# A hybrid decoder trunk in one core: the input loaded in halves with its first products begun block by block, and the last tile's final norm done token by token

## The chip, the core and the metric

One core of a Trainium2 chip runs the whole program in one launch. The metric is the device time of one execution in microseconds; the time of a kernel is the median over its executions. Engines are named as in the profile: PE is TensorE, DVE is VectorE, ACT is ScalarE, POOL is GpSimd, SP is SyncE, which here only issues DMAs.

## What is computed

A step of a two-layer trunk over 512 prompt tokens and 8 sample tokens of width 1024, all in float32. Each layer is a recurrent mixer followed by a retrieval layer (PEER), and the result goes through one more norm:

```python
def rmsnorm(x, w):
    xf = x.astype(jnp.float32)
    y = xf * lax.rsqrt(jnp.mean(xf * xf, axis=-1, keepdims=True) + EPS)
    return (y * w.astype(jnp.float32)).astype(x.dtype)
```

Layer 0 does norm, an input projection, gated DeltaNet and Mamba-2 side by side, an output projection and a residual add. Layer 1 does the same with GLA. In each layer the retrieval picks, for every token, 128 experts (8 heads, 16 each) out of 16384. The row of an expert holds a vector u and a vector v of 1024 numbers each. The token's output is the sum over its experts of gate * gelu(u . h) * v, which is added to x.

## The kernel before

**Layout.** Everything before the retrieval is kept with the channels on the partitions: `xT` is (128, 8, 520), 8 blocks of 128 channels by 512 prompt and 8 sample tokens. The tokens are worked in two pairs of tiles: columns 0 to 255, and 256 to 519. A projection (`gemm`, PE) reads weight blocks of 128x1024 (0.52 MB each), which SP loads into a ring of 3 slots, and makes 8 products per block, each of them two MATMUL instructions in the profile. The results stand in PSUM banks 2 and 3 by turns; block b waits until the bank of block b-2 was read (`gemm_free`). ACT and DVE read them out.

**Start.** SP issues 12 loads (`NLOADS`), all counted by one semaphore, `params`: the masks (of which `ones` and `ident` are two planes), the whole of `xT`, and the small tensors, the last of them `a_log`; then the weight blocks. PE, ACT and DVE wait for all 12 (L982, L1322, L1906). Then comes the first norm, over `xT[:, :, 0:256]`: ACT squares 8 channel blocks (L1090), DVE adds them up one by one (L1414), PE sums over the partitions by a product with `ones` (L564), ACT takes the root (L1103), DVE its reciprocal and then scales the 8 channel blocks into `hT` (L1424). The first projection waits for all 8 (`h_ready`, L627).

**Order of work.** From then on a unit is one tile of 128 tokens in one layer; 8 units follow one another, the last being tile 3 of layer 1. A unit is a loop over 128 picks (136 in tile 3's, which take the 8 sample tokens in as 8 further picks). Pick g: POOL gathers 128 rows of 8 KB by an indirect DMA into one of 7 ring slots, DVE makes the dot product with `htok` (L2168), ACT the gate and a diagonal matrix of it, PE two products (half a row of v each, 4 MATMUL instructions) that add into PSUM banks 0 and 1. A slot is free again when PE is done (`v_done`). In units 0 to 5 some picks' v is added by DVE instead. The mixers of later tiles, the choice of experts and the final norms of earlier tiles are cut into pieces, each with a due pick, and run between the picks (`front`, `choose`). In the last unit nothing of this is left but the picks.

**End of a unit.** ACT copies the sum out of PSUM into `otok`, PE turns it by 8 transposes (L1076), for tile 3 also the sample tokens' columns by 8 small ones (L1080), and DVE adds it to `xT` (L2142). The final norm is again squares, sums, product, root, reciprocal, 8 scalings into `y_out`, and POOL stores that with one DMA (L527). For tile 3 with the sample tokens (136 columns, `FINAL[2]`) all of this comes after the last pick, as nothing else is left. POOL then waits for all stores.

## Time and profile before

| | |
|---|---|
| median of 3 runs | 3461.0 us (3457.2 to 3465.04) |
| the profiled execution's own time | 3458.52 us |
| its span in the profile | 3456.7 us |
| TensorE's mean granted clock | 0.938 of full speed |
| busy | PE 2853.8 (83%), DVE 2331.4 (67%), ACT 1210.4 (35%), POOL 1265.8 (37%) |
| DMA | 1225.42 MB, mean 355 GB/s; DMA engines' busy share by fortieths of the span: 4204697998999899999999999999999899999996 |
| chain that ended last | PE 44%, DMA 27%, DVE 16%, ACT 5%, issue 4% |

The profile is of one execution, whose span leaves out 1.8 us that its own time has. A busy time is of one engine; a share of the chain says how much of the span the end of the kernel hung on that engine's work or on a transfer. "Idle before" in a row of the timeline is how long the engine had nothing to do before it, and what ended that.

### The profile page before, as it was taken

Reading aid. Unit: us, or ns where it says so; the run is one execution under the profiler, and the core shown is the slowest. Engines: PE = TensorE matmul, PEld = TensorE weight load, DVE = VectorE, ACT = ScalarE, POOL = GpSimd, SP = SyncE. Lnnn points to the kernel's source line nnn. Section 1 sums busy time; section 2 is a strip of 40 time slices with the busy share of each in tenths; the row PEclk is TensorE's granted clock in tenths of the full one; section 3 lists DMA queues with packets and bytes.
Section 4 is the critical chain, followed back from the end, with each engine's and each line's share of the span. In section 5 each row is a group of like instructions: output and inputs, shape, how many; then the busy total and the mean of one; then the engine's idle time right before and its main releaser. Section 6 shows DMA issues by size and latency. Waiting matters only on the chain.

```text
span 3456.7 us, 31768 instructions
## 1 busy us (share of the span) xinstructions
PE 2853.8 (83%) x9796; PEld 1642.4 (48%) x9796; DVE 2331.4 (67%) x5015; ACT 1210.4 (35%) x3536; POOL 1265.8 (37%) x1102
## 2 busy tenths in 40 slices
PE   7879897888997788797988898787788787787886
PEld 6767664555564256454642356354355232322222
DVE  3453788786767888687566787766667776755444
ACT  3211355332333343433333432432323343333333
...
DMA  4204697998999899999999999999999899999996
GB/s 148 80 1 143 238 359 300 358 365 362 407 413 420 367 406 382 384 386 387 411 421 421 389 406 381 361 343 412 369 413 420 349 419 421 386 422 419 421 422 268
DMA packets 183660, 1225.42 MB, mean 355 GB/s; under 512 B 21185, under 2 KB 21585, under 8 KB 48194
## 3 DMA queue, kind: packets, MB, share of 16 engines
...
## 4 chain that ended last, share of the span: by engine, by line
PE 44%; DMA 27%; DVE 16%; ACT 5%; issue 4%; DVEq 2%; POOL 1%; SPq 0%; POOLq 0%; ACTq 0%
PE ps L562 43%; DMA ring<-in_uv,picked 25%; DVE ring L2168 5%; DVE otok L2133 1%; ACT diag L1088 1%; ACT scratch L1088 1%; DVEq L1974 1%; POOL ring L547 1%; DVE scratch L1937 1%; ACT gated L1088 1%; DMA out_o_gla<-scratch 1%; ACT L1088 1%; ACT act_v L1088 1%; DVE scratch L1941 0%; DVE scratch L1955 0%
## 5 line engine op out<-in xcount | busy, mean ns | idle before, releaser
L562 PE MATMUL ps<-ring,diag 128*128 128x512 f32 (+1 forms) x3380 | 1712.9, 639 | 380.4 <-ACT diag L1088 371.4
L547 POOL DMA_INDIRECT ring<-in_uv,picked x1024 | 1181.2, 1154 | 1806.5 <-PE ps L562 1281.7
L2168 DVE SCALAR_TENSOR_TENSOR ring<-ring,htok 128x1024 f32<-128x1024 f32 x1024 | 1250.3, 1228 | 666.0 <-DMA ring<-in_uv,picked 659.9
L562 PEld LDWEIGHTS ps<-ring,diag 128*128 128x128 f32 (+1 forms) x3380 | 621.8, 198 | 1231.9 <-ACT diag L1088 687.3
L1088 ACT ACTIVATE act_v<-pre 128x1 f32<-128x1 f32 x1040 | 212.0, 204 | 1725.6 <-DVE ring L2168 1716.5
L562 PE MATMUL ps<-hT,wring 128*128 128x256 f32 (+1 forms) x3200 | 749.4, 389 | 38.6 <-DVE hT L1438 11.4
L562 PEld LDWEIGHTS ps<-hT,wring 128*128 128x128 f32 x3200 | 617.9, 194 | 210.7 <-issue 94.6
L1088 ACT ACTIVATE diag<-masks,gated 128x128 f32<-128x128 f32 x829 | 334.4, 403 | 28.4 <-PE ps L562 1.5
L1088 ACT ACTIVATE gated<-act_v,gates 128x1 f32<-128x1 f32 x1024 | 304.3, 297 | 33.4
L562 PEld LDWEIGHTS ps<-scratch 128*128 128x128 f32 (+2 forms) x1428 | 191.3, 197 | 110.6 <-issue 67.1
L562 PE MATMUL ps<-scratch 128*128 128x128 f32 (+5 forms) x1428 | 210.5, 293 | 40.3 <-DVE scratch L1583 16.7
L2133 DVE SCALAR_TENSOR_TENSOR otok<-ring,gated,otok 128x1024 f32<-128x1024 f32 x189 | 242.3, 1282 | 0.0
L1088 ACT ACT_TABLE_LOAD x99 | 127.0, 1283 | 3.4 <-DVEq L1405 1.7
L1088 ACT ACTIVATE scratch<-ps 128x256 f32<-128x256 f32 (+6 forms) x112 | 62.6, 564 | 115.2 <-PE ps L562 115.0
L1473 DVE SCALAR_TENSOR_TENSOR keep<-keep,conv_w 128x256 f32<-128x256 f32 x120 | 58.1, 485 | 54.1 <-ACT keep L1088 46.0
L2168 DVE DVE_READ_ACCUMULATOR ring<-ring,htok 128x1 f32 x1024 | 85.5, 83 | 0.0
L471 POOL TENSOR_TENSOR scratch<-scratch,masks 128x512 f32<-128x512 f32 x18 | 25.7, 1436 | 161.5 <-DVE scratch L1560 150.0
L562 PE MATMUL ps<-keep,masks 8*128 8x256 f32 (+7 forms) x116 | 31.2, 401 | 52.8 <-DVE keep L1422 50.4
L1088 ACT ACTIVATE keep<-ps 128x264 f32<-128x264 f32 (+4 forms) x146 | 42.9, 324 | 80.7 <-PE ps L562 80.7
L1088 ACT ACTIVATE keep<-xT 128x256 f32<-128x256 f32 (+3 forms) x80 | 31.1, 391 | 74.2 <-DVE xT L1456 58.4
L562 PEld LDWEIGHTS ps<-keep,masks 8*128 8x128 f32 (+1 forms) x116 | 21.2, 206 | 66.9 <-DVE keep L1422 38.9
L1088 ACT ACTIVATE keep<-ps,conv_b,conv_w 128x256 f32<-128x256 f32 x40 | 22.4, 561 | 75.3 <-PE ps L562 75.3
...
## 6 DMA issues: line engine op xcount, KB each, us to landing
...
ring<-in_uv,picked POOLq DMA_INDIRECT x1024
scratch<-in_keys POOLq DMA_DIRECT2D x4, 1024.0 KB, 11.5
...
scratch<-in_s_ssm POOLq DMA_DIRECT2D x1, 2048.0 KB, 17.2
```

The costliest lines, as they stand in the source:

```text
L471: pool.tensor_tensor(nl[:, (6 * m + l - 1) % 4, :].rearrange("p (h i) -> p h i", h=4), nmat, mask4(LEVEL0 + l), ALU.mult).then_inc(sem(f"n ...
L547: pool.indirect_dma_start(out=ring[:, g % RING, :], out_offset=None, in_=io["uv"][L], in_offset=bass.IndirectOffsetOnAxis(ap=index, axis=0 ...
L562: return pe.matmul(out, lhsT, rhs, start=start, stop=stop)
L1088: return act.activation(out, in_, func, **k)
L1473: last = stt(y, x[:, 3 - s:259 - s], conv_w[:, j, 3 - s:4 - s], y, MUL, ADD)
L1937: tt(e, posf[R, H].rearrange("p h (k a) -> p (h k) a", a=1).to_broadcast(full), each(iota[:, :] if step == 8 else row_at).to_broadcast(ful ...
L1974: dve.drain()
L2133: last = stt(otok[:, :], ring[:, g % RING, D:2 * D], weight, otok[:, :], MUL, ADD)
L2168: stt(x, x, 1.0, h, MUL, MUL, accum_out=pre[:, g % SMALL:g % SMALL + 1]).then_inc(sem("dotted"), 1)
```

## The change

**At the start** only the 256 columns of x that the first norm reads are loaded first, in two loads of four channel blocks with a semaphore each; then `ones` and `ident`, and `ln`, on a semaphore of their own. Three weight blocks follow, and behind them the other 11 loads, among them the rest of x and of the masks. The wait for those (`params`) moves: ACT has it after the first root, DVE after the first scaling, PE ahead of the first gate product (beside block 3). ACT takes a root of a constant first. The squares of the first norm are shared by ACT (blocks 0, 2, 4, 6, 7) and DVE (1, 3, 5); DVE adds three pairs, PE sums five operands in PSUM instead of one. In block 0 of the first projection each product waits for the scaling of its own channel block.

**At the end** tile 3's final norm is done with the tokens on the partitions. During the last unit, behind its pick 20, PE turns tile 3 of `xT` back and ACT copies it to `last_y`. The sample tokens' columns are turned and added to `xT` behind the third-last and second-last picks. After the last pick DVE adds the two halves of the sum from PSUM to `last_y` (the first as soon as PE's first half of the last pick is done), squares and sums each row in the same instruction, ACT takes a root of one column, and DVE scales by it and by a row of weights (`ln_row`), which SP loads after the last weight block into all partitions. SP stores the two halves, 128 tokens by 512, into a new output `o_yt`. The 8 sample tokens keep the old layout: squares, eight small products, root, and a store of 128x8 pieces of 8 numbers by POOL. The other norms and the other 7 units stay as they were.

```diff
-NLOADS = 12
+NLOADS = 11
...
-        y_out = [fin.take(KD, n) for n in (256, 128, 136)]
-        FINAL = ((0, 256, 6, 784), (256, 128, 7, 908), (384, 136, 8, END - 1))
+        y_out = [fin.take(KD, n) for n in (256, 128, NS_TOK)]
+        FINAL = ((0, 256, 6, 784), (256, 128, 7, 908))
+
+
+        first_sq = sq_qk
+        last_y = fin.take(D)
+        ln_row = fin.take(D)
+        s_sq = fin.take(KD, NS_TOK)
+        s_root = fin.take(NS_TOK)
+        row_sum = fin.take(4)
+        x_s = xT[:, :, TILE_AT[S]:TILE_AT[S] + NS_TOK]
+        ROWS_AT = FIRST[7] + 20
+        LAST_NO = 10
 
         def norm_no(k, p):
...
         def _(sp):
-            n = 0
-            for dst, src in ((masks[:, :, :], io["masks"]), (xT[:, :, :], io["xT"]), (ln[:, :, :], io["ln"]),
-                             (conv_w[:, :, :], io["conv_w"]), (conv_b[:, :], io["conv_b"]),
-                             (small_w[:, :, :], io["small_w"]), (glr_w[:, :, :], io["glr_w"]),
-                             (head_w[:, :], io["head_w"]), (gate2[:, :], io["gate2"]), (pack[:, :], io["pack"]),
-                             (small_b[:, :], io["small_b"].to_broadcast([P, 16])),
-                             (a_log[:, :], io["a_log"].to_broadcast([P, 12]))):
-                sp.dma_start(dst, src).then_inc(sem("params"), 16)
-                n += 1
-            assert n == NLOADS
+            for h in range(2):
+                sp.dma_start(xT[:, 4 * h:4 * h + 4, 0:256], io["xT"][:, 4 * h:4 * h + 4, 0:256]).then_inc(sem(f"x_loaded{h}"), 16)
+            sp.dma_start(masks[:, 0:2, :], io["masks"][:, 0:2, :]).then_inc(sem("base_loaded"), 16)
+            sp.dma_start(ln[:, :, :], io["ln"]).then_inc(sem("base_loaded"), 16)
+
+            def params():
+                n = 0
+                for dst, src in ((conv_w[:, :, :], io["conv_w"]), (conv_b[:, :], io["conv_b"]),
+                                 (small_w[:, :, :], io["small_w"]), (small_b[:, :], io["small_b"].to_broadcast([P, 16])),
+                                 (a_log[:, :], io["a_log"].to_broadcast([P, 12])), (masks[:, 2:, :], io["masks"][:, 2:, :]),
+                                 (xT[:, :, 256:T], io["xT"][:, :, 256:T]), (glr_w[:, :, :], io["glr_w"]),
+                                 (head_w[:, :], io["head_w"]), (gate2[:, :], io["gate2"]), (pack[:, :], io["pack"])):
+                    sp.dma_start(dst, src).then_inc(sem("params"), 16)
+                    n += 1
+                assert n == NLOADS
+
             for name, p in ORDER:
                 for j in range(BLOCKS[name]):
                     b = FIRST_BLOCK[name, p] + j
+                    if b == WSLOTS:
+                        params()
                     if b >= WSLOTS:
                         sp.wait_ge(sem("gemm_done"), b - WSLOTS + 1)
                     block_no = IN_ORDER[p][j] if name == "even_in" else j
                     sp.dma_start(wring[:, b % WSLOTS, :, :].rearrange("p k c -> p (k c)"), io["weights"][BASE[name] + block_no])\
                         .then_inc(sem(f"w_loaded{b % WSLOTS}"), 16)
+            sp.wait_ge(sem("h_ready"), norm_no(3, 1) + 1)
+            sp.dma_start(ln_row, io["ln_row"].to_broadcast([P, D])).then_inc(sem("base_loaded"), 16)
+            for h in range(2):
+                sp.wait_ge(sem("h_ready"), LAST_NO + 2 + h)
+                sp.dma_start(io["o_yt"][:, 512 * h:512 * h + 512], last_y[:, 512 * h:512 * h + 512]).then_inc(sem("rows_stored"), 16)
+            sp.wait_ge(sem("rows_stored"), 32)
 
         @block.gpsimd
...
             front.upto(END - 1)
+            pool.wait_ge(sem("h_ready"), LAST_NO + 1)
+            pool.dma_start(io["o_y"][:, :, TILE_AT[S]:TILE_AT[S] + NS_TOK], y_out[2]).then_inc(sem("y_stored"), 16)
             pool.wait_ge(sem("conv_stored"), 32)
...
+            def first_norm():
+                pe.wait_ge(sem("base_loaded"), 32)
+                for c in (0, 1, 2, 3, 5):
+                    if c in (0, 2):
+                        pe.wait_ge(sem("first_squares"), c // 2 + 1)
+                    elif c in (1, 3):
+                        pe.wait_ge(sem("other_squares"), c // 2 + 1)
+                    else:
+                        pe.wait_ge(sem("other_squares"), 3)
+                    last = mm(ps[:, 2, 0:256], ones, first_sq[:, c, :], c == 0, c == 5)
+                last.then_inc(sem("ssq_ready"), 1)
+
             def early_sum():
...
-                pe.wait_ge(sem("h_ready") if norm is not None else sem("mix_ready"),
-                           norm_no(norm, p) + 1 if norm is not None else 2 * (name == "odd_out") + p + 1)
+                first = (name, p) == ("even_in", 0)
+                if not first:
+                    pe.wait_ge(sem("h_ready") if norm is not None else sem("mix_ready"),
+                               norm_no(norm, p) + 1 if norm is not None else 2 * (name == "odd_out") + p + 1)
...
+                            pe.wait_ge(sem("first_scaled"), c + 1)
+                        elif first and j == 0:
+                            pe.wait_ge(sem("h_ready"), 1)
                         last = mm(ps[:, 2 + b % 2, 0:n], wring[:, b % WSLOTS, c, :], hT[:, c, 0:n], c == 0, c == KD - 1)
...
+            def last_rows(g):
+                if g == ROWS_AT:
+                    for c in range(KD):
+                        last = pe.transpose(ps[:, 4 + c // 4, (c % 4) * P:(c % 4 + 1) * P],
+                                            xT[:, c, TILE_AT[3]:TILE_AT[3] + P], ident)
+                    last.then_inc(sem("htok_mm"), 1)
+                if g == SAMPLE_G[1][-1] + 5:
+                    sample_columns(1)
+
+            def sample_columns(L):
+                pe.wait_ge(sem("sample_out"), L + 1)
+                for c in range(KD):
+                    last = pe.transpose(ps[:, 2, c * NS_TOK:(c + 1) * NS_TOK], htok[0:NS_TOK, 2, c * P:(c + 1) * P],
+                                        ident[0:NS_TOK, 0:NS_TOK])
+                if L:
+                    last.then_inc(sem("out_mm"), 1)
+                return last
 
             def choice():
...
+                                last.then_inc(sem("v_done"), 1)
                         last.then_inc(sem("v_done"), 1)
                     if j < COUNT[u] - 1:
                         front.upto(min(g + LEAD, FIRST[u + 1] - 1))
                         choose.upto(min(g + LEAD, FIRST[u + 1] - 1))
+                    last_rows(g)
+                if u == len(UNITS) - 1:
+                    continue
```

ACT's and DVE's sides of the same (their common waits for `params` and `eps_ready` ahead of the mixers are gone; `norm(4, p)` now runs for p = 0, 1 only):

```diff
+            def first_norm():
+                act.wait_ge(sem("eps_ready"), 1)
+                f(act_v[:, 0:1], eps[:, 0:1], ACT.Sqrt)
+                for c in (0, 2, 4, 6, 7):
+                    act.wait_ge(sem(f"x_loaded{c // 4}"), 16)
+                    f(first_sq[:, c, :], xT[:, c, 0:256], ACT.Square).then_inc(sem("first_squares"), 1)
+                root(0, 0)
+                act.wait_ge(sem("params"), 16 * NLOADS)
 
...
             front.upto(END - 1)
+            act.wait_ge(sem("added"), len(UNITS))
+            f(s_sq, x_s, ACT.Square).then_inc(sem("squares_ready"), 1)
+            act.wait_ge(sem("ssq_ready"), LAST_NO + 1)
+            f(s_root, ps[:, 3, 0:NS_TOK], ACT.Sqrt, scale=1.0 / D, bias=eps[:, 0:1]).then_inc(sem("root_ready"), 1)
+            act.wait_ge(sem("squares_added"), KD * (squares_no(4, 1) + 1) + 1)
+            f(row_sum[:, 2:3], row_sum[:, 2:3], ACT.Sqrt, scale=1.0 / D, bias=eps[:, 0:1]).then_inc(sem("root_ready"), 1)
 
...
+            def first_norm():
+                for c in (1, 3, 5):
+                    dve.wait_ge(sem(f"x_loaded{c // 4}"), 16)
+                    last = tt(first_sq[:, c, :], xT[:, c, 0:256], xT[:, c, 0:256], MUL)
+                    if c < 5:
+                        last.then_inc(sem("other_squares"), 1)
+                for i, c in enumerate((4, 6, 7)):
+                    dve.drain()
+                    dve.wait_ge(sem("first_squares"), 3 + i)
+                    last = tt(first_sq[:, 5, :], first_sq[:, 5, :], first_sq[:, c, :], ADD)
+                last.then_inc(sem("other_squares"), 1)
+                dve.wait_ge(sem("base_loaded"), 32)
+                yield from scale_rows(0, 0)
+                dve.wait_ge(sem("params"), 16 * NLOADS)
 
...
+                    if (k, p) == (0, 0) and c < KD - 1:
+                        last.then_inc(sem("first_scaled"), 1)
...
+            def last_tile():
+                halves = [slice(512 * h, 512 * h + 512) for h in range(2)]
+                dve.wait_ge(sem("htok_ready"), max(HTOK) + 1)
+                for h, v in enumerate(halves):
+                    if h == 0:
+                        dve.wait_ge(sem("v_done"), TURNED[-1])
+                    else:
+                        dve.wait_ge(sem("v_done"), TURNED[-1] + 1)
+                    y = last_y[:, v]
+                    tt(y, y, ps[:, h, :], ADD)
+                    dve.drain()
+                    stt(otok[:, v], y, 1.0, y, MUL, MUL, accum_out=row_sum[:, h:h + 1])
+                dve.drain()
+                tt(row_sum[:, 2:3], row_sum[:, 0:1], row_sum[:, 1:2], ADD).then_inc(sem("squares_added"), 1)
+                dve.wait_ge(sem("root_ready"), LAST_NO + 1)
+                dve.reciprocal(s_root, s_root)
+                dve.drain()
+                tt(y_out[2], x_s, s_root.rearrange("p (a b) -> p a b", a=1).to_broadcast([P, KD, NS_TOK]), MUL)
+                dve.drain()
+                tt(y_out[2], y_out[2], ln[:, 4, :].rearrange("p (c a) -> p c a", a=1).to_broadcast([P, KD, NS_TOK]), MUL)\
+                    .then_inc(sem("h_ready"), 1)
+                dve.wait_ge(sem("root_ready"), LAST_NO + 2)
+                dve.reciprocal(row_sum[:, 3:4], row_sum[:, 2:3])
+                dve.drain()
+                dve.wait_ge(sem("base_loaded"), 48)
+                for v in halves:
+                    y = last_y[:, v]
+                    stt(y, y, row_sum[:, 3:4], ln_row[:, v], MUL, MUL).then_inc(sem("h_ready"), 1)
 
             front, choose = Strand(mixers()), Strand(choice())
...
+                        dve.wait_ge(sem("out_mm"), len(UNITS))
+                        add_sample().then_inc(sem("added"), 1)
             front.upto(END - 1)
+            last_tile()
```

## Rows read from the trace of the kernel before

**Rows 1.** Windows: stretch, its length; PE, PEld, DVE, ACT, POOL busy; clock, DMA share, GB/s.
```profile
2640.00:2650.00 10.00, 7.97 (x35) 4.40 (x33) 6.20 (x10) 4.29 (x12) 4.75 (x5) 1.00 1.01 419
2800.00:3200.00 400.00, 314.54 (x678) 117.71 (x679) 252.77 (x569) 155.84 (x491) 164.79 (x158) 0.98 1.00 413
3200.00:3430.00 230.00, 194.16 (x402) 65.26 (x402) 113.01 (x184) 83.32 (x277) 89.22 (x86) 1.00 0.99 410
```

**Rows 2.** Chain that ended last, first 60 us: start us, us, what.
```profile
7.58 5.71 DMA a_log<-in_a_log
...
24.69 35.51 PE ps L562 x171
```

**Rows 3.** Timeline of the start: start us, us, engine, line, op, xcount, [idle before].
```profile
0.75 0.38 SPq L430 DMA_DIRECT2D masks<-in_masks  x1
...
7.58 0.44 SPq L430 DMA_DIRECT2D a_log<-in_a_log  x1
...
13.31 3.78 ACT L1088 ACTIVATE keep<-xT 128x256 f32<-128x256 f32 x8 [10.33 <-DMA a_log<-in_a_log]
...
17.82 1.19 PE L562 MATMUL ps<-keep,masks 128*128 128x256 f32 x2 [17.82 <-DVE keep L1422]
19.04 0.48 ACT L1088 ACTIVATE keep<-ps,eps 128x256 f32<-128x256 f32 x1 [0.66 <-PE ps L562]
19.55 1.75 DVE L1432 RECIPROCAL keep<-keep 128x256 f32<-128x256 f32 x1 [1.89 <-ACT keep L1088]
21.38 3.25 DVE L1438 SCALAR_TENSOR_TENSOR hT<-xT,ln,keep 128x256 f32<-128x256 f32 x8
...
24.69 15.75 PE L562 MATMUL ps<-hT,wring 128*128 128x256 f32 x64 [5.68 <-DVE hT L1438]
...
30.12 0.57 ACT L1088 ACTIVATE keep<-ps,conv_b,conv_w 128x256 f32<-128x256 f32 x1 [10.60 <-PE ps L562]
```

**Rows 4.** Windows of the start, two us each: same columns as rows 1.
```profile
0.00:2.00 2.00, 0.00 (x0) 0.00 (x0) 0.56 (x12) 0.30 (x1) 0.34 (x5) 1.00 0.31 43
2.00:4.00 2.00, 0.00 (x0) 0.00 (x0) 0.00 (x0) 0.98 (x1) 0.00 (x0) 1.00 0.80 298
4.00:6.00 2.00, 0.00 (x0) 0.00 (x0) 0.00 (x0) 0.00 (x0) 0.00 (x0) 1.00 1.11 452
```

**Rows 5.** Windows of 3 us in block 0 and in a later block.
```profile
24.60:27.60 3.00, 2.91 (x7) 2.37 (x8) 0.10 (x2) 0.00 (x0) 0.00 (x0) 1.00 0.00 0
30.60:33.60 3.00, 3.00 (x16) 2.64 (x15) 1.45 (x3) 0.45 (x4) 0.00 (x0) 1.00 0.54 175
```

**Rows 6.** Windows around one weight load alone, issued at 30.11 us.
```profile
31.00:31.50 0.50, 0.50 (x4) 0.45 (x3) 0.44 (x1) 0.03 (x1) 0.00 (x0) 1.00 1.00 180
...
32.50:33.00 0.50, 0.50 (x4) 0.44 (x3) 0.16 (x1) 0.00 (x0) 0.00 (x0) 1.00 0.48 189
```

**Rows 7.** Timeline of the end, same columns as rows 3.
```profile
3424.04 1.23 DVE L2168 SCALAR_TENSOR_TENSOR ring<-ring,htok 128x1024 f32<-128x1024 f32 x1 [1.24 <-DMA ring<-in_uv,picked]
...
3426.51 1.23 DVE L2168 SCALAR_TENSOR_TENSOR ring<-ring,htok 128x1024 f32<-128x1024 f32 x1 [1.23 <-DMA ring<-in_uv,picked]
...
3428.79 1.98 PE L562 MATMUL ps<-ring,diag 128*128 128x512 f32 x4 [0.48 <-ACT diag L1088]
...
3432.92 0.66 PE L1080 MATMUL ps<-masks,htok 8*128 8x8 f32 x8
3433.61 1.22 DVE L2146 TENSOR_TENSOR xT<-xT,ps 128x1024 f32<-128x1024 f32 x1 [5.88 <-PE ps L1080]
3434.75 0.21 DVE L2149 TENSOR_TENSOR xT<-xT,ps 128x64 f32<-128x64 f32 x1
...
3441.11 2.25 DVE L1438 SCALAR_TENSOR_TENSOR keep<-xT,ln,keep 128x136 f32<-128x136 f32 x8
3443.67 0.92 POOL L527 DMA_DIRECT2D out_o_y<-keep  x1 [29.17 <-DVE keep L1438]
```

**Rows 8.** DMA issues after 3430 us: what, queue, count, KB, us to landing.
```profile
out_o_y<-keep POOLq DMA_DIRECT2D x1, 544.0 KB, 3.9
```

63 lines of the change are left out of this document (36 added, 27 removed).

## The prediction

> **What bounds the kernel now.** The chain of waits, followed back from the end, shows where the first microseconds go: in its first 60 us it waits for the last of the twelve loads, `a_log`, until 13.3 us, and then for the first norm, before PE starts the first projection at 24.69 and is on the chain without a gap [rows 2]. The timeline fills that in: nothing but loads until 13.31, then squares and sums, PE's one product at 17.82, root 19.04, reciprocal 19.55, scalings 21.38 to 24.63 [rows 3]. PE has idled 5.68 us before its first product of weights. So each microsecond by which that product starts sooner is one off the time, if what follows keeps up.
>
> The middle is long, and its DMA engines are full: 413 and 410 GB/s at a share of 1.00 and 0.99 in the last 600 us, and 1.01 at 2640 us [rows 1]. Little of this is touched. It follows the start by semaphores, not by the clock, so a head start passes through it; but bytes added in it cost time.
>
> The end is read from the timeline again. PE's last products run from 3428.79 to 3430.77; copy, transposes, adds and norm follow one after another, and POOL issues the last store at 3443.67 [rows 7]. It lands 3.9 us later, at 3447.57 [rows 8]; the 9.1 us from there to the end of the span hold nothing that the rows show, and I leave them as they are.
>
> **The start, step by step.** *Loads.* The two halves of x (1.05 MB), two mask planes (0.13) and `ln` (0.02) are 1.20 MB. Before, the DMA engines moved 2 us x 43 GB/s + 2 us x 298 GB/s = 0.68 MB in the first four microseconds, and 452 GB/s after that [rows 4], so 1.20 MB were through at 4 + 0.52/0.452 = 5.15 us. The new pieces are of 1 KB, the old ones of 6 to 17 KB a partition. A weight load alone, in 4 KB pieces, was issued at 30.11, its first bytes came about 1.0 later and its last at about 32.8 [rows 6]: 0.52 MB in 1.7 us, 300 GB/s. At that rate, with the first issue at 0.75 [rows 3], the second half of x is there at 1.75 + 1.05/0.3 = 5.25 and the rest at 5.75. I take 5.8 us for `base_loaded`. The ends are 5.2 and 9.0 (all three weight blocks, 1.57 MB more, served alongside: 2.77 MB at 380 GB/s, between the two rates, from 1.75).
> *Squares.* After 5.25, ACT has three (0.47 each, from 3.78 for eight [rows 3]) and DVE one more add: done near 7.1. That is beside PE, whose four other operands are ready and wait for `ones`.
> *The sum in PSUM.* Before, one product, two MATMULs, took 1.19 us [rows 3]. PE works there at half rate: in block 0 it ran 7 MATMULs in 2.91 us, later 16 in 3.00, counted where they touch the window [rows 5], and block 0 took 5.43 us (24.69 to 30.12). The view grants 1.00 in both stretches, so it is the durations that tell; they fit the 1.2 GHz level after idling and the 2.4 GHz one once busy. Five products are 1.19 + 8 x 0.43 = 4.6 us: 5.8 to 10.4. This is a term that the change adds: 3.4 us more of PE than before, on the path.
> *Root to first product.* The distances of before: 19.01 to 21.38 for root and reciprocal, 0.48 for the first scaling, 0.04 to PE [rows 3], together 2.9. The first product starts at 13.3 and not at 24.69: **11.4 us sooner**. Of this 2.8 come from waiting for one scaling and not for eight (24.69 - 21.90). The other seven, 0.41 apart, stay ahead of PE's 0.86 per product at half rate.
> *What stands behind.* Block 0 takes 5.43 as before, to 18.7. The first three weight blocks are issued before the other loads and land by about 10. The wait for `params` now stands in ACT ahead of the reading of block 0 (18.7), in DVE ahead of the convolutions, in PE ahead of block 3's gate products. On SP eighteen issues come first where twelve took until 8.02; at that pace the last one is out near 11.5, and it lands 5.7 later if it goes like `a_log` (7.58 to 13.29) [rows 2, 3]: 17.2. By bytes: 4.8 MB at 380 GB/s are through at 14.4. Either is before 18.7, so the wait costs nothing. If it were later, PE would stall only beyond 21.2: ACT needs 1.0 us to free a bank, and PE has block 1, 3.45 us long, to run meanwhile. SP's next weight load waits for the end of block 0, later than 11.5.
> *Bounds of this part.* Gain of 11.4; at worst 3.2 less (`base_loaded` at 9.0) and 1.4 less (all 16 MATMULs of block 0 at half rate, 6.9); at best 2.3 more (the sum at full rate, 2.3 us instead of 4.6) and 1.6 more (block 0 at full rate, where DVE's 3.84 bounds it).
>
> **The middle.** `ln_row` is read 128 times over, 0.52 MB through engines that are at 1.01 of their share at 2640 us, at 419 GB/s [rows 1], where it would be issued: **1.2 us lost** (nothing if it slips into a gap). PE's 8 transposes behind pick 20 (about 1.1 us) meet 0.5 us of idle time per pick and a ring of seven slots; ACT's copy of 1.0 us is likewise hidden in a period of 2.5. Without those gathers queued ahead, the two would cost a microsecond.
>
> **The end.** *The sample columns.* A pick's period is 2.47 (3424.04 to 3426.51 between two dots [rows 7]), so PE's third-last group of products ends two periods before the last, at 3430.77 - 4.94 = 3425.83; 8 small transposes of 0.66 behind it end at 3426.5. DVE waits for them in front of the last dot product, adds (0.21), and starts that dot at 3426.8 instead of 3426.51: 0.3 lost. What is queued behind on DVE is only this dot, but ACT and PE hang on it.
> *Last products* 3429.1 to 3431.1, the first half done at 3430.2. *DVE* per half: add 0.61 (half of 1.22), square with sum 0.61 + 0.08, a drain 0.05: two halves 2.7, to 3432.9; their sum 0.1. *ACT's root* of one column 0.3: 3433.3. Beside it DVE does the samples' reciprocal and two small products (0.21 each): 3433.65; their squares, sums and root on ACT and PE ran while DVE was in its halves. Reciprocal 0.1 and two scalings of 0.61: 3434.4 and 3435.0. *Stores.* SP's second: a weight load takes 2.7 us from issue to last byte for 0.52 MB [rows 6], half the bytes 0.85 less, and 0.6 for the receipt: 3437.5. POOL's, issued at 3433.7 and taken at the 3.9 of before [rows 8]: 3437.6. Landing at 3437.6 and not 3447.57: **10.0 us sooner**. Gone are the copy to `otok`, 8 transposes, an add of 1.22, 8 squares with adds, a reciprocal over 136 columns and 8 scalings (2.25). Bounds: 11 with no delay and stores of 3.3; 8.3 if the samples' 1024 pieces of 32 bytes take 1.7 longer (below).
>
> **Sum.** 11.4 + 10.0 - 1.2 = 20.2. The profiled execution had 3458.5 us of its own: 3438.3. The median of the runs stands 2.5 above it: 3440.8, so 3441.
>
> **Two rules of the Trainium skill.** The page TensorE: Matmul & The Clock Gate (Part 1) says that the throttled clock is the default and that activity releases it, by time and not by a number of matmuls. By that the five products of the norm can themselves release it, and block 0 would find full rate: 3439.2, a rival below. DMA: Bandwidth & Descriptors (Specifications) has transfers below 512 B done as a read-modify-write, which speaks against the samples' new store; no row here prices that, and before its pieces were of 544 B.
>
> **The rivals.**
> A, **the clock is up for block 0.** For: PE is busy 4.6 us in the norm where before it was 1.2. Against: it then idles 2.9 us, and by [rows 5] it was at half rate after 5.7. Block 0 is 3.84 long: 3439.2.
> B, **the loads are served together**, weights beside x and masks, and `base_loaded` comes at 9.0: 3444.0. For: the loads of before overlap at the end, as `a_log`, a load of 6 KB, took 5.7 us with weights issued behind it [rows 2, 3].
> C, **the samples' store ends last.** 1024 pieces, 64 per DMA engine; at 0.03 us each more than now, 1.7 us: 3442.5.
> D, **the block-by-block start does nothing**, as PE starts only when all is scaled, for whatever reason: 2.8 back, 3443.6.
> E, **slower: the wait for `params` takes the place of the old one.** ACT cannot read block 0 before all 11 loads are in. PE stalls from 21.2 us on, one for one; the kernel is no faster from 21.2 + 20.2 = 41.4, and slower by 0.2% from 48; with the loads at 50 the time is 3461 + 8.6 = 3469.6. Against it stand the 17.2 and the 14.4 us above.
>
> **How the numbers follow.** 0.2% is 7 us, about what a measurement can tell from no change here. Chances: forecast 0.60, A 0.12, B 0.10, C 0.08, D 0.05, E 0.03, and 0.02 for gains lost in ways unknown. All but the last two are faster by more than 7 us. The low end is both best bounds of the start (3.9 below) and 3 of the runs' scatter of 4: 3434. The high end is B or D with block 0 at half rate, 3445.4 at most, and again 3 of scatter: 3448.
>
> **What would show it.** First MATMUL with `wring` near 13.3 and first reading of block 0 near 18.7, with no wait of ACT for a load after it; ten MATMULs with `ones` from 5.8 to 10.4, their length telling A from the forecast. The last products end near 3430.77 - 11.4 + 1.2 + 0.3 = 3420.9, and the last landing is 6.5 us after them, not 16.8. Wrong it would be if `base_loaded` came after 9.0, if the first wait in ACT after the root were a load beyond 21, or if the last store landed over 9 us after the last product.

## The result and the profile after

| | before | after |
|---|---|---|
| median of the runs | 3461.62 us (3457.2 to 3465.04, 4 runs) | 3429.83 us (3425.36 to 3435.68, 4 runs) |
| the profiled execution: own time, span | 3458.52, 3456.7 | 3425.36, 3423.6 |
| TensorE's mean granted clock in it | 0.938 | 0.937 |
| busy: PE, DVE, ACT, POOL | 2853.8, 2331.4, 1210.4, 1265.8 | 2858.6, 2329.0, 1199.4, 1277.4 |
| DMA | 1225.42 MB | 1225.96 MB, mean 358 GB/s |

The ratio is 0.9906, with an interval from 0.9888 to 0.9925: 31.8 us gone, where 20.2 were forecast. Faster was right. The number was not: 3441 was predicted, and 3429.83 lies below the range, which ended at 3434.

**The start.** The timeline of after, same columns as [rows 3]:

```profile
2.33 0.71 SPq L440 DMA_DIRECT2D ln<-in_ln  x1
...
4.88 0.72 ACT L1161 ACTIVATE scratch<-xT 128x256 f32<-128x256 f32 x2 [2.65 <-DMA xT<-in_xT]
...
6.32 1.03 ACT L1161 ACTIVATE scratch<-xT 128x256 f32<-128x256 f32 x3 [0.71 <-DMA xT<-in_xT]
...
6.97 4.60 PE L592 MATMUL ps<-scratch,masks 128*128 128x256 f32 x10 [6.97 <-DMA ln<-in_ln]
...
11.03 0.36 SPq L449 DMA_DIRECT2D pack<-in_pack  x1
11.62 0.47 ACT L1161 ACTIVATE keep<-ps,eps 128x256 f32<-128x256 f32 x1 [4.26 <-PE ps L592]
12.23 1.75 DVE L1536 RECIPROCAL keep<-keep 128x256 f32<-128x256 f32 x1 [3.98 <-ACT keep L1161]
14.05 3.25 DVE L1542 SCALAR_TENSOR_TENSOR hT<-xT,ln,keep 128x256 f32<-128x256 f32 x8
...
14.69 6.24 PE L592 MATMUL ps<-hT,wring 128*128 128x256 f32 x20 [3.11 <-DVE hT L1542]
17.91 0.06 DVE L1825 MEMSET keep<- 128x6 f32 x1 [0.60 <-DMA pack<-in_pack]
...
20.17 0.56 ACT L1161 ACTIVATE keep<-ps,conv_b,conv_w 128x256 f32<-128x256 f32 x1 [8.08 <-PE ps L592]
```

The first product starts at 14.69, 10.0 us sooner than in [rows 3]. The ten MATMULs with `ones` take 4.60, and block 0 takes 5.48 (14.69 to 20.17). The chain says what came late: it goes through the load of `ln` (start us, us, what):

```profile
2.33 4.55 DMA ln<-in_ln
```

The loads of `params` cost nothing: DVE waits 0.60 us for the last of them, `pack`, until 17.91, and ACT reads block 0 at 20.17 with PE's product as the releaser.

**The clock and the middle.** Windows of after, columns as in [rows 1]:

```profile
14.68:15.08 0.40, 0.40 (x2) 0.36 (x3) 0.40 (x2) 0.00 (x0) 0.00 (x0) 1.00 1.09 366
15.08:18.49 3.41, 3.41 (x10) 2.71 (x9) 2.29 (x7) 0.00 (x0) 0.00 (x0) 0.50 0.32 98
18.49:20.17 1.68, 1.68 (x9) 1.47 (x9) 0.00 (x0) 0.00 (x1) 0.00 (x0) 1.00 0.00 0
2650.00:2660.00 10.00, 7.73 (x16) 2.71 (x16) 9.84 (x40) 3.52 (x12) 4.22 (x5) 1.00 1.01 403
```

Block 0 begins at full rate: its first two MATMULs start 0.29 us apart, where those of before start 0.59 apart. So after the 4.6 us of the norm the clock had come up. Then 0.50 of it is granted from 15.08 to 18.49, the level of 1.2 GHz, behind PE's 3.11 us without work, and in those 3.41 us only 10 MATMULs are touched; behind them 9 in 1.68 us. The half rate that before has in its block 0 [rows 5] came back, a little later. At 2650 us the DMA engines are at 1.01 of their share, as in [rows 1].

**The end.** The timeline of after, beside [rows 7]:

```profile
3401.12 1.23 DVE L2304 SCALAR_TENSOR_TENSOR ring<-ring,htok 128x1024 f32<-128x1024 f32 x1 [1.24 <-DMA ring<-in_uv,picked]
...
3402.84 0.66 PE L1051 MATMUL ps<-masks,htok 8*128 8x8 f32 x8
...
3403.54 0.22 DVE L2257 TENSOR_TENSOR xT<-xT,ps 128x64 f32<-128x64 f32 x1 [1.18 <-PE ps L1051]
3403.67 1.22 DVE L2304 SCALAR_TENSOR_TENSOR ring<-ring,htok 128x1024 f32<-128x1024 f32 x1
...
3405.95 1.98 PE L592 MATMUL ps<-ring,diag 128*128 128x512 f32 x4 [0.54 <-ACT diag L1161]
...
3409.32 0.69 DVE L2270 SCALAR_TENSOR_TENSOR otok<-keep 128x512 f32<-128x512 f32 x1
...
3410.29 0.29 ACT L1161 ACTIVATE keep<-keep,eps 128x1 f32<-128x1 f32 x1 [0.37 <-DVE keep L2272]
...
3411.48 1.42 DVE L2286 SCALAR_TENSOR_TENSOR keep<-keep 128x512 f32<-128x512 f32 x2
3411.61 0.91 POOL L581 DMA_DIRECT2D out_o_y<-keep  x1 [20.05 <-DVE keep L2278]
3412.26 1.00 SPq L467 DMA_DIRECT2D out_o_yt<-keep  x2
```

The last dot product comes 2.55 us behind the one before it, where it was 2.47: the sample tokens' transposes and add delay it by less than 0.1. From the end of the last products (3407.93) POOL issues the samples' store 3.7 us later and SP the two halves 4.3 and 5.0 us later. How the stores land stands in the view of the DMA issues after 3408 us (columns as in [rows 8]):

```profile
out_o_yt<-keep SPq DMA_DIRECT2D x2, 256.0 KB, 2.8
out_o_y<-keep POOLq DMA_DIRECT2D x1, 32.0 KB, 2.8
```

The samples' store of 1024 pieces of 32 bytes needs 2.8 us; the old one, of 1024 pieces of 544 bytes and so of 17 times the bytes, needed 3.9. The 1.7 us on top of the old time that rival C feared are not there; what small pieces cost by themselves these two stores can't tell. (The Trainium skill, DMA: Bandwidth & Descriptors, Specifications, has pieces under 512 B done as a read-modify-write; if it happens here, it hides in the 2.8.) From the end of the last products to the end of the execution's own time it is 17.43 us, where it was 3458.52 - 3430.77 = 27.75: 10.3 sooner. Of these the stores bring 9.0: the last packet ends 7.42 us after the last product, where it was 16.39. The other 1.3 lie behind the last packet, where the span goes on for 8.23 us and not for 9.57.

So the two ends bring 10.0 + 10.3, and 31.8 - 20.3 = 11.5 us are more than they account for; between the two profiled executions, which lie 33.2 apart, it is 12.8. The traces place it. From the first product (24.69, 14.69) to the last dot product (3426.51, 3403.67) before took 3401.8 us and after 3389.0: **the middle is 12.8 us shorter**, though hardly a line of it was changed. I matched the 1040 dot products of one trace with those of the other. After is ahead by 11.3 us at the 125th of them, and by 18.1 at the 131st. Between these two lies this stretch of PE's timeline, of before:

```profile
801.04 3.57 PE L562 MATMUL ps<-keep,scratch 128*128 128x1 f32 x16 [7.59 <-DMA scratch<-in_s_dn]
804.47 3.76 PE L562 MATMUL ps<-ring,diag 128*128 128x512 f32 x4
808.02 6.83 PE L562 MATMUL ps<-keep,scratch 128*128 128x1 f32 x32
814.71 3.76 PE L562 MATMUL ps<-ring,diag 128*128 128x512 f32 x4
818.26 3.41 PE L562 MATMUL ps<-keep,scratch 128*128 128x1 f32 x16
```

and the same stretch of after:

```profile
790.06 3.57 PE L592 MATMUL ps<-keep,scratch 128*128 128x1 f32 x16 [8.08 <-DMA scratch<-in_s_dn]
793.49 3.57 PE L592 MATMUL ps<-ring,diag 128*128 128x512 f32 x4
796.89 3.85 PE L592 MATMUL ps<-keep,scratch 128*128 128x1 f32 x32
800.61 3.42 PE L592 MATMUL ps<-ring,diag 128*128 128x512 f32 x4
803.87 1.84 PE L592 MATMUL ps<-keep,scratch 128*128 128x1 f32 x16
```

PE idles 8 us for the sample tokens' states (`in_s_dn`), and then makes 64 products of one column each, with a pick's four MATMULs after the 16th and after the 48th of them (the sample tokens' DeltaNet). In before everything here takes its long time: 16 one-column products 3.41 to 3.57, a pick's four 3.76. The granted clock is 0.50 from 796.1 to 826.8. In after it is at half level for 10.2 us and once more for 3.4, and between and behind them 32 products take 3.85 where before had 6.83, and the last 16 take 1.84. The saving there, 6.8 us, is more than half of the 12.8; 1.3 came before it and 4.7 in the 2500 us behind it. Nothing in that stretch was edited; the change could have shortened it only by moving it against the clock. That was the question of the runs.

### The profile page after: what moved, and what is told of

Read it like the earlier page. It is cut to its first block, busy times and chain, and to the rows that moved or that the text cites. A ratio compares the mean times of both kernels' runs of the same rounds, so it can differ in the third digit from the quotient of the medians.

```text
span 3423.6 us, 31787 instructions
## 1 busy us (share of the span) xinstructions
PE 2858.6 (83%) x9818; PEld 1645.7 (48%) x9818; DVE 2329.0 (68%) x5008; ACT 1199.4 (35%) x3527; POOL 1277.4 (37%) x1102
## 2 busy tenths in 40 slices
DMA packets 186077, 1225.96 MB, mean 358 GB/s; under 512 B 21281, under 2 KB 23857, under 8 KB 50738
## 4 chain that ended last, share of the span: by engine, by line
PE 43%; DMA 28%; DVE 17%; ACT 5%; issue 4%; DVEq 2%; POOL 1%; SPq 0%; ACTq 0%; POOLq 0%
PE ps L592 42%; DMA ring<-in_uv,picked 27%; DVE ring L2304 6%; DVE otok L2238 1%; ACT scratch L1161 1%; DVEq L2079 1%; ACT diag L1161 1%; DVE scratch L2042 1%; POOL ring L575 1%; ACT gated L1161 1%; ACT L1161 1%; DMA out_o_gla<-scratch 1%; ACT act_v L1161 1%; DVE scratch L2083 1%; DVE scratch L2046 0%
## 5 line engine op out<-in xcount | busy, mean ns | idle before, releaser
L1161 ACT ACTIVATE gated<-act_v,gates 128x1 f32<-128x1 f32 x1024 | 301.7, 295 | 33.2
L592 PE MATMUL ps<-scratch 128*128 128x128 f32 (+5 forms) x1428 | 213.7, 296 | 38.2 <-DVE scratch L1689 16.1
L1579 DVE SCALAR_TENSOR_TENSOR keep<-keep,conv_w 128x256 f32<-128x256 f32 x120 | 58.2, 485 | 51.3 <-ACT keep L1161 43.3
L592 PE MATMUL ps<-keep,masks 8*128 8x256 f32 (+7 forms) x128 | 31.0, 375 | 28.3 <-DVE keep L1511 25.8
L592 PEld LDWEIGHTS ps<-masks,keep 128*128 128x128 f32 x288 | 39.0, 204 | 10.8 <-issue 10.7
## 6 DMA issues: line engine op xcount, KB each, us to landing
scratch<-in_keys POOLq DMA_DIRECT2D x4, 1024.0 KB, 11.6
out_o_dn<-scratch POOLq DMA_DIRECT2D x1, 2048.0 KB, 12.8
```

What stands on the lines that cost most here:

```text
L592: return pe.matmul(out, lhsT, rhs, start=start, stop=stop)
L1161: return act.activation(out, in_, func, **k)
L1579: last = stt(y, x[:, 3 - s:259 - s], conv_w[:, j, 3 - s:4 - s], y, MUL, ADD)
```

## The experiments

Two theories. **Luck:** the middle is not of one length in any kernel, as the half-clock stretches fall where they fall, and the change is worth its two ends, 20 us less 1.4. **Shift:** the change itself, by its start or by its end, makes the middle shorter. All kernels below are the changed one with the edit shown. Each kernel's time is the median of its runs, beside that of before on the same chip in the same series, which was 3458.95, 3459.72, 3462.07 and 3459.99 in the four series.

### One half of the change at a time

`before_again` is the kernel before, unedited. `front_only` puts the old end back, `tail_only` the old start, as the diff of the change has them:

```diff
 front_only
-        y_out = [fin.take(KD, n) for n in (256, 128, NS_TOK)]
-        FINAL = ((0, 256, 6, 784), (256, 128, 7, 908))
+        y_out = [fin.take(KD, n) for n in (256, 128, 136)]
+        FINAL = ((0, 256, 6, 784), (256, 128, 7, 908), (384, 136, 8, END - 1))
 ...
 tail_only
-NLOADS = 11
+NLOADS = 12
 ...
         def squares_no(k, p):
-            return sum_no(k, p) - 1
+            return sum_no(k, p)
```

> The kernel before, unchanged, for a second trace of it. Three theories stand for the 12.8 us that the changed kernel gained between the first product and the last pick. L (luck): where TensorE's clock falls and rises differs from execution to execution, and this trace loses or keeps its half-speed stretch at 800 to 826 us at random; then this run's stretches lie elsewhere than the first trace's and its time is anywhere from 3445 to 3465. S (start): the gain in the middle follows from the earlier start; then this trace repeats the first, 3457 to 3465, with 30 us at half clock between 800 and 850. T (tail part): the same as S for this run.

> Only the start of the change (loads in halves, shared squares, first products block by block); the end is that of before. My sums as corrected by the trace: the first product starts 10.0 us sooner. S: the middle's 12.8 come with it, so 22 to 23 us less than before, near 3439. T: 10 us less, near 3451.5. L: 10 less on the mean, with a scatter of 10 between executions.

> Only the end of the change (last tile token by token, ln_row, transposes beside the picks); the start is that of before. From the trace of the changed kernel the last landing came 9 us sooner after the last product. S: 9 less, and 0 to 1.2 back for ln_row: 8 to 9 us less than before, near 3453. T: 21 to 22 less, near 3440. L: 8 to 9 less with a scatter of 10.

Measured: `before_again` 3455.13 in one run. `front_only` 3440.78, ratio 0.9955 (0.9939 to 0.9971), 18 us. `tail_only` 3448.61, ratio 0.9975 (0.9959 to 0.999), 10 us. In the traces `front_only`'s first product comes at 14.50 and its middle is 3388.8 us, as short as in after; `tail_only`'s is 3403.3 and `before_again`'s 3399.0. That spoke for a shift by the start. It spoke against one by the end. But `before_again` spoke against both: the shift theories wanted its trace to repeat the 30 us at half clock, and between 780 and 850 us its longest piece at half level is 13.7 us.

### The same kernel again

`after_again` and `after_third` are the changed kernel with no edit at all.

> The changed kernel again, for a second trace and a narrower interval: 30 to 33 us less than before. S and T: the trace has its half-clock stretches where the first had them until 850 us (some 15 us of half clock between 800 and 850, counted on the time of before), and the lead over before steps from 11 to 18 us there. L: the step is at another place or absent.

> The changed kernel once more, on the chip of the three others and with a third trace. L: its time is 20 to 28 less than before, its middle (last pick counted from the first product) between 3385 and 3400 us, and its lead made at places unlike those of the first two traces.

Measured: 3436.95, ratio 0.9944 (0.9926 to 0.9963), and 3437.0, ratio 0.9934 (0.9921 to 0.9947). The middles are 3397.1 and 3401.7 us, against 3401.8 and 3399.0 in the two traces of before. `after_again` has before's long stretch at half level; its PE timeline:

```profile
781.79 3.57 PE L592 MATMUL ps<-keep,scratch 128*128 128x1 f32 x16 [7.75 <-DMA scratch<-in_s_dn]
785.22 3.76 PE L592 MATMUL ps<-ring,diag 128*128 128x512 f32 x4
788.77 6.83 PE L592 MATMUL ps<-keep,scratch 128*128 128x1 f32 x32
```

So the same program shows both. The first four runs of the change, with a mean of 3430.2, lay 7 us below the eleven of these two kernels, with 3437.1. That is 2.8 standard errors of the difference, which chance makes in about 2 of 100 cases; it is called luck below because the same program did not repeat it in eleven runs, and nothing more shows that it was.

### The start held back

If the head start passes through, and nothing else comes of it, a start held back by a few microseconds costs just these. `late10` and `late2` let SP wait, ahead of its first load, for DVE, which first takes reciprocals of a tile that nobody reads (five, and one):

```diff
+            sp.wait_ge(sem("go"), 1)
             for h in range(2):
                 sp.dma_start(xT[:, 4 * h:4 * h + 4, 0:256], io["xT"][:, 4 * h:4 * h + 4, 0:256]).then_inc(sem(f"x_loaded{h}"), 16)
...
+                dve.memset(otok[:, 0:256], 1.0)
+                for n in [256, 256, 256, 256, 256]:
+                    dve.drain()
+                    dve.reciprocal(otok[:, 0:n], otok[:, 0:n])
+                signal("go")
```

> The changed kernel, but SP sends its first load only after DVE has done a memset and five reciprocals of 128x256 on an unused tile (some 9.5 us): everything behind is as in the changed kernel and later by that. The five traces so far agree that the new start is worth 10.0 us at the first product, and that the two ends of the change and ln_row's load add up to 20.2 less 1.0 to 1.4. They also gained 5 to 13 us more between first product and last pick with the new start than with the old. Theory P (place in time): that extra comes from starting sooner; here it vanishes, the time is 3459 - 20 + 9.5 = 3449. Theory F (form): the new start leaves something behind (other order of loads) that helps the middle whenever it happens: 3434.5 + 9.5 = 3444. Theory L (luck): the extra is the drift of TensorE's half-speed stretches from execution to execution and its mean is near 0: 3449, with executions from 3440 to 3457, and stretches placed unlike those of the first trace.

> The same with one reciprocal: some 2.1 us later than the changed kernel. P: the middle depends on the place in time, so its length changes by several microseconds either way, and the place of the half-speed stretches with it. F and L: 2.1 us slower than the changed kernel on the mean, 3436.5.

Measured: `late10` 3449.53, ratio 0.9966 (0.9948 to 0.9983). Its first product is at 24.78, where before has it, and its time is within 1 us that of `tail_only`, whose start is the old one: the order of the loads shows no worth beyond the moment of the first product. The intervals leave room for some: `late10`'s reaches down to 3441.7, and so takes in the 3444 of the theory of form. `late2` 3442.86, ratio 0.9948 (0.9929 to 0.9966), with the first product at 17.75 and a middle of 3410.1. It lies above what was expected, but its runs spread from 3433.0 to 3452.2.

### The parts of the new start

`all_scaled` lets PE wait for all eight scalings:

```diff
-                        if first and j == 0 and c < KD - 1:
-                            pe.wait_ge(sem("first_scaled"), c + 1)
-                        elif first and j == 0:
+                        if first and j == 0 and c == 0:
                             pe.wait_ge(sem("h_ready"), 1)
```

> The changed kernel, but the first product waits for all eight scalings (h_ready), not for its own. If block by block is worth what the rows of before say, the first product starts 2.7 to 2.8 us later in the trace (at 17.4) and block 0 is as long as before; on the time the same 2.7, within the scatter. If PE was cold anyway and rival D holds, there is no difference.

Its timeline:

```profile
13.68 3.25 DVE L1540 SCALAR_TENSOR_TENSOR hT<-xT,ln,keep 128x256 f32<-128x256 f32 x8
17.08 10.29 PE L592 MATMUL ps<-hT,wring 128*128 128x256 f32 x35 [5.88 <-DVE hT L1540]
```

From the first scaling to the first product it is 3.40 us, where after has 0.64: **block by block is worth 2.8 us** at the first product, as predicted. Block 0 itself takes 6.3 us here and 5.5 in after. The time was 3438.75, ratio 0.9944 (0.993 to 0.9959).

`one_load` loads the two halves of x with one DMA:

```diff
-            for h in range(2):
-                sp.dma_start(xT[:, 4 * h:4 * h + 4, 0:256], io["xT"][:, 4 * h:4 * h + 4, 0:256]).then_inc(sem(f"x_loaded{h}"), 16)
+            sp.dma_start(xT[:, :, 0:256], io["xT"][:, :, 0:256]).then_inc(sem("x_loaded0"), 16)
```

> The changed kernel with x's 256 columns in one load and one semaphore instead of two halves. If the halves pay: squares all start when the second half is there (6.3 us), ACT's five take 1.9 more, but PE's products wait for ones at 6.9 and need four squares only by then; squares 0 to 3 come at 6.7 to 7.2, so PE starts 0.2 later at most and the last sum operand (DVE's) at 9.3 is still before PE needs it (10.4). First product 14.7 to 14.9 as in the changed kernel: the halves are hidden. If instead they pay, it is 1.4 later, 16.1. Time within the scatter of the changed kernel.

```profile
6.46 1.64 ACT L1160 ACTIVATE scratch<-xT 128x256 f32<-128x256 f32 x5 [4.23 <-DMA xT<-in_xT]
...
7.12 4.61 PE L591 MATMUL ps<-scratch,masks 128*128 128x256 f32 x10 [7.12 <-DMA ln<-in_ln]
...
14.84 12.50 PE L591 MATMUL ps<-hT,wring 128*128 128x256 f32 x49 [3.11 <-DVE hT L1541]
```

The first square comes 1.6 us later, the first product 0.15. PE waits for `ln` all the same, and five squares are made beside its sum: from PE's start at the sum to the first product it is 7.72 us here and 7.72 in after. **The halves with waits of their own bring nothing** as long as `base_loaded` comes last; time 3443.18, ratio 0.9941 (0.9919 to 0.9963).

`ones_between` puts the load of `ones` between the halves, and PE no longer waits for `ln`:

```diff
                 sp.dma_start(xT[:, 4 * h:4 * h + 4, 0:256], io["xT"][:, 4 * h:4 * h + 4, 0:256]).then_inc(sem(f"x_loaded{h}"), 16)
-            sp.dma_start(masks[:, 0:2, :], io["masks"][:, 0:2, :]).then_inc(sem("base_loaded"), 16)
+                if h == 0:
+                    sp.dma_start(masks[:, 0:2, :], io["masks"][:, 0:2, :]).then_inc(sem("ones_loaded"), 16)
...
-                pe.wait_ge(sem("base_loaded"), 32)
+                pe.wait_ge(sem("ones_loaded"), 16)
```

> The changed kernel with the two mask planes loaded between the two halves of x, on a semaphore of their own that PE waits for; ln stays behind. PE then starts its five products when square 0 and ones are there, near 5.3, not 6.97. If the chain is ones, then PE at half clock (my reading), the sum ends 1.2 to 1.7 sooner: the fifth operand needs block 7's square (7.4 + 0.4) and DVE's adds, 8.7 to 9.3, and PE ends at 10.1 to 10.4 instead of 11.57; first product at 13.1 to 13.5. If the squares set the end, it stays at 14.7.

```profile
5.12 3.75 PE L593 MATMUL ps<-scratch,masks 128*128 128x256 f32 x8 [5.12 <-ACT scratch L1162]
7.37 1.03 ACT L1162 ACTIVATE scratch<-xT 128x256 f32<-128x256 f32 x3 [2.08 <-DMA xT<-in_xT]
...
9.35 1.22 PE L593 MATMUL ps<-scratch,masks 128*128 128x256 f32 x2 [0.48 <-DVE scratch L1523]
...
13.68 13.55 PE L593 MATMUL ps<-hT,wring 128*128 128x256 f32 x53 [3.11 <-DVE hT L1543]
```

PE begins at 5.12 and four of its five operands are through by 8.9, but the second half of x now lands at 7.37 and not at 6.32, and the fifth operand waits for its squares and adds. The first product comes 1.0 sooner than in after: the wait has moved from `ln` to the load that was pushed back. One pair of traces is a rough measure of it: with the start of the change the first product comes at 14.13 to 14.69 in four traces (after, its two repeats, `front_only`), with this start at 12.76 to 14.06 in six, 0.9 sooner on the mean. Time 3436.29, ratio 0.993 (0.9905 to 0.9955).

`pe_one` takes the four products away that the change adds: DVE adds all squares, PE makes one product:

```diff
-                for c in (0, 1, 2, 3, 5):
...
-                    last = mm(ps[:, 2, 0:256], ones, first_sq[:, c, :], c == 0, c == 5)
-                last.then_inc(sem("ssq_ready"), 1)
+                pe.wait_ge(sem("other_squares"), 1)
+                mm(ps[:, 2, 0:256], ones, first_sq[:, 5, :]).then_inc(sem("ssq_ready"), 1)
```

> The changed kernel, but DVE adds all the squares and PE makes one product of two MATMULs instead of five of ten. If the 4.6 us of PE at half clock are the term that the change added to the path, this takes 3.4 off PE and puts four adds of 0.48 on DVE's chain: the last add ends near 10.0, the sum near 11.2 instead of 11.57, first product 14.3. If PE's ten MATMULs were hidden behind the squares, it would be slower, 15.5 or later.

```profile
9.40 1.19 PE L592 MATMUL ps<-scratch,masks 128*128 128x256 f32 x2 [9.40 <-DVE scratch L1523]
...
13.70 13.53 PE L592 MATMUL ps<-hT,wring 128*128 128x256 f32 x54 [3.11 <-DVE hT L1542]
```

The first product comes at 13.70, 1.0 sooner than in after and 0.4 sooner than in the earliest of the four traces with that start. So the sum in PSUM is a cost, as the prediction had it: here DVE's adds are through sooner than the four products at half rate. Time 3442.05, ratio 0.9929 (0.9897 to 0.9961).

### The load of `ln_row`

`row_on_chip` is `ones_between` without that load: in the last unit PE spreads the weights of the norm by eight products, and ACT copies them out.

```diff
-            sp.wait_ge(sem("h_ready"), norm_no(3, 1) + 1)
-            sp.dma_start(ln_row, io["ln_row"].to_broadcast([P, D])).then_inc(sem("base_loaded"), 16)
...
+                if g == ROWS_AT + 5:
+                    for c in range(KD):
+                        last = mm(ps[:, 6 + c // 4, (c % 4) * P:(c % 4 + 1) * P], ln[:, 4, c:c + 1].to_broadcast([P, P]), ident)
+                    last.then_inc(sem("row_mm"), 1)
```

> As ones_between, and ln_row is not loaded: behind pick 25 of the last unit PE makes it by eight products of 128x128 out of ln, and ACT copies it. All seven traces with the load lose 1.3 to 1.8 us against the trace of before between 2600 and 2660 us, the two without it 0 and gain 0.2; so here nothing is lost there. Together with ones_between some 2.8 us less than the changed kernel: 3432.5 on the mean, with the scatter of 5 between executions.

> row_on_chip once more, beside the kernel with the added products: by its trace the first product is 0.6 to 1.0 sooner than in the changed kernel and 1.3 to 1.8 us of ln_row's load are saved, so 2 to 2.8 less than the changed kernel's 3435.2 (mean of 15): 3433, some 25 less than before.

Measured: 3435.68, ratio 0.9922 (0.9894 to 0.9949), and the same kernel again 3435.52, ratio 0.9933 (0.991 to 0.9955). The price of the load shows in the traces. Between the 728th and the 736th dot product (2620.6 and 2641.7 us in before) each of the ten traces with the load falls behind before by 1.3 to 1.6 us (after 1.3, `pe_one` 1.6). The seven without it lose next to nothing there (`before_again` and `front_only` 0.0, `row_on_chip` and `row_again` 0.1, the three of the next section 0.2 to 0.4). In the time of the whole kernel 1.4 us can't be told: the 13 runs without the load, which start sooner too, average 3435.8, the 15 of the changed kernel 3435.2 and its eleven repeats alone 3437.1.

### The clock held up

`awake` is `row_on_chip` with 26 products of `ident` with masks, which nobody reads: ten ahead of PE's wait for the states, and two ahead of each of the eight groups of one-column products.

```diff
+                def keep_busy(n):
+                    for _ in range(n):
+                        mm(ps[:, 5, 256:512], ident, masks[:, 2:4, :].rearrange("p a b -> p (a b)"))
+                keep_busy(10)
                 pe.wait_ge(sem("dn_states"), 16)
                 for h in range(4):
                     yield slot(2 + h)
+                    keep_busy(2)
```

`awake_b` and `awake_c` are the same kernel again.

> row_on_chip with products that nobody reads (256 columns, into a free half of a PSUM bank) in the samples' stage of layer 0: ten ahead of PE's wait for the samples' states (7.6 us idle before), two ahead of each of the eight groups of one-column products. The stretch from dot 120 to dot 136 took 56.8 to 58.9 us in five traces, with TensorE back at full clock within 14 us of 772, and 61.3 to 65.6 in nine, with 14 to 31 us at half clock there. If the half clock makes the difference: full clock there and 56 to 60 us in all three of these runs, though PE has up to 11 us more work at that place. If it only goes with it: 61 to 66 or more, as work is added.

> The same kernel for a second trace; same expectation: dot 120 to 136 in 56 to 60 us if the clock makes it, 61 or more if not.

> The same kernel for a third trace; same expectation: dot 120 to 136 in 56 to 60 us if the clock makes it, 61 or more if not.

```profile
790.44 1.13 PE L591 MATMUL ps<-masks 128*128 128x256 f32 x4 [2.51 <-DMA scratch<-in_s_dn]
791.41 2.14 PE L591 MATMUL ps<-keep,scratch 128*128 128x1 f32 x16
...
797.46 1.84 PE L591 MATMUL ps<-keep,scratch 128*128 128x1 f32 x16
```

PE idles 2.5 to 3.7 us ahead of that stretch and not 7 or 8, and no piece at half clock there is longer than 6.8 us in the three traces, where the longest is 10.2 to 30.7 us in the fifteen others. So the fillers work on the clock. They bring no time: from the 121st to the 137th dot product it is 60.0, 60.6 and 62.6 us, between the 56.8 of after and the 63.9 of before, and the kernel took 3435.59 (ratio 0.9935, 0.9911 to 0.9958), one run each of the others 3438.74 and 3436.34.

What the clock is worth there can be read from the fifteen traces without fillers. The time from the 121st to the 137th dot product follows the time at half clock within it, 13.7 to 37.8 us, with a correlation of 0.98: 51.8 us and 0.36 us more for each at half clock, no trace being over 1.5 off that line. By the line the three filled stretches (8.9, 11.6 and 17.8 us at half clock) would take 55.0, 56.0 and 58.2; they take 4.5 to 5.0 us more, which is what the fillers' own PE time costs. That is an estimate from traces side by side: no experiment changed the clock alone.

### All traces side by side

"First" is the start of the first product, "middle" the time from there to the last dot product, "121 to 137" the time between these two dot products, "half" how much of the middle the clock was granted at 0.50 (the view shows 1.00 in before's block 0, which ran at half rate, so a kernel's first half-rate time is not in it). The two columns behind are the gain over before (difference of medians within a series), and what the ends account for: 24.28 (mean of the three old starts) less the first product, 10.3 for the new end, 1.4 off where `ln_row` is loaded.

| kernel | first | middle | 121 to 137 | half | gain | ends |
|---|---|---|---|---|---|---|
| before | 24.69 | 3401.8 | 63.9 | 409.6 | | |
| before_again | 24.15 | 3399.0 | 61.3 | 436.9 | | |
| tail_only | 24.01 | 3403.3 | 65.2 | 447.1 | 10.3 | 9.2 |
| late10 | 24.78 | 3407.0 | 65.6 | 450.6 | 10.2 | 8.4 |
| after | 14.69 | 3389.0 | 56.8 | 416.4 | 31.8 | 18.5 |
| after_again | 14.30 | 3397.1 | 64.8 | 423.2 | 22.0 | 18.9 |
| after_third | 14.13 | 3401.7 | 58.6 | 474.2 | 22.7 | 19.1 |
| front_only | 14.50 | 3388.8 | 56.9 | 399.4 | 18.2 | 9.8 |
| late2 | 17.75 | 3410.1 | 64.5 | 471.0 | 16.9 | 15.4 |
| all_scaled | 17.08 | 3399.8 | 58.9 | 442.0 | 21.0 | 16.1 |
| one_load | 14.84 | 3409.1 | 64.5 | 454.0 | 18.9 | 18.3 |
| ones_between | 13.68 | 3402.6 | 65.0 | 450.6 | 25.8 | 19.5 |
| pe_one | 13.70 | 3412.3 | 63.1 | 464.2 | 20.0 | 19.5 |
| row_on_chip | 14.06 | 3394.9 | 57.1 | 413.0 | 26.4 | 20.5 |
| row_again | 12.90 | 3400.8 | 57.1 | 419.5 | 24.5 | 21.7 |
| awake | 13.52 | 3402.6 | 60.0 | 430.1 | 24.4 | 21.1 |

The start of a kernel sets its "first", and the end is as fixed: from the last dot product to the end of the own time it is 21.3 to 21.7 us in every trace with the new end and 32.0 to 32.6 in the three with the old one. All scatter sits between. The middle goes from 3388.8 to 3412.3 us, whichever start the kernel has, and follows the time at half clock: over these and the two repeats of `awake` (3404.3 with 429.0, 3400.7 with 460.8) the correlation is 0.72, which leaves about half of the scatter to something else. Among 60 runs of the kernel before, time and mean granted clock go together as well (-0.70; clocks from 0.926 to 0.937). None of these 60 had a mean clock as high as the 0.938 of before's profiled execution.

## Why the prediction was right and wrong

**The two ends were right: 20.2 predicted, about 19 found** (10.0 + 10.3 - 1.4). That it came so near is in part luck, as the 1.3 us behind the last packet were not in the prediction and made up for the stores. By terms:

- *`base_loaded`*: 5.8 predicted, 6.97 found (6.6 to 6.9 in the two repeats and `front_only`). This is the one term of the start that was mis-sized by over 0.2. The last of the four loads, 0.02 MB issued at 2.33, took 4.55 us; I had put it by bytes, with the halves at 300 GB/s. The second half of x came 1.1 us late too (6.32, 5.25 predicted).
- *The sum in PSUM*: 4.6 predicted, 4.60 found, and a cost (without the four added products `pe_one` has its first product 0.4 to 1.0 sooner).
- *Root to first product*: 2.9 predicted, 3.1 found. *First product*: 13.3 predicted, 14.69 found, so 10.0 and not 11.4 gained.
- *Block 0*: 5.43 predicted, 5.48 found. Rival A (full clock in block 0) is out by its price, and half right in its mechanism. The sum did free the clock: in after, `after_again`, `front_only`, `late2` and `one_load` block 0 starts at full rate, and 0.50 is granted from 0.4 to 0.8 us into it, for 3.41 us, behind PE's idle 3.1 us, as the objection to A had it. In `after_third` the 0.50 begins at 13.84, ahead of the first product. Before's block 0 has its half-rate time at its front, and so the length is the same. The Trainium skill's rule (TensorE: Matmul & The Clock Gate, Part 1: activity releases the throttle, idling sets it again) agrees with both.
- *Block by block*: 2.8 predicted, 2.8 in `all_scaled` at the first product. Rival D is out.
- *`params`*: 17.2 predicted, 17.9 found, ahead of the reading of block 0 at 20.17. Rival E is out. Rival B (9.0) is out, though the late `base_loaded` is a step in its direction.
- *`ln_row`*: 1.2 predicted, 1.3 to 1.6 found, and 0 to 0.4 without the load.
- *The delay of the last dot*: 0.3 predicted, under 0.1 found. *The end*: 10.0 with the delay in it predicted, 10.3 found, by two misses that cancel. The stores bring 9.0: the halves go out 4.3 and 5.0 us after the last product and need 2.8, where the working had 3.3, 3.9 and some 2.5. And the stretch behind the last packet, which I left as it was, is 1.3 shorter (8.2 in every trace with the new end, 9.6 in `before_again` and `front_only` too; why is not known). Rival C is out, as POOL's store lands at 3414.4, ahead of SP's, which end at about 3415.5.

**The step that failed** is the sentence on the middle: "It follows the start by semaphores, not by the clock, so a head start passes through it". The head start does pass through, on average: held back by 10.5 us, `late10` gains 12 less than the changed kernel's repeats (10.2; 22.0 and 22.7). But the sentence made of the middle a constant, and of the scatter "3 of the runs' scatter of 4", taken from three runs. The middle is PE work and gathers whose time goes with how long the clock is down, and it differs by 23 us between 18 traces. Single runs carry that: before's 64 have a mean of 3460.1 and a standard deviation of 6.3, the changed kernel's 15 one of 3435.2 and 5.2. By these the change is worth 25 us. But four of the 15 are the ones whose low value called for the repeats; by the eleven others, with 3437.1, **the change is worth 23 us, 3 either way**. The two later measurements of it, 3436.95 and 3437.0, lie inside the predicted range. The first, 3429.83, is below it, and some 7 of its 31.8 us did not come again with the same program. A range that had known this scatter would have been wider on both sides.

**The shift theory** does not stand in the traces, for a shift of the size of 12.8 us. The middle is 3401.4 us in the mean of the three traces with the old start, and 3401.1 in that of the twelve with the new one and no fillers. The end part makes it no shorter either (`tail_only` 3403.3).

**What stays open.** The gain exceeds what the ends account for in every line of the table, by 0.5 to 8.4 us, apart from the first measurement 3.4 on average. Of each alone but one the interval takes that in (`front_only`'s begins at 10.0, where the ends account for 9.8), but all with one sign do not look like chance, though they share four medians of before and so are not independent. The runs say the same: 23 us, 3 either way, against the 19 of the ends, so some 4 us of the gain have no cause shown. With the old or the late start the excess is 1.1 and 1.8 (`tail_only`, `late10`), in the eleven others 3.7 on average: a small shift by the start is not ruled out. The traces, one per kernel, can't show an effect of 3 us in a middle that scatters by 23. And it wasn't tried why the clock falls for 30.7 us in one execution and for 10.2 in another.
